# Two-layer hybrid encoder on one core: where the first layer's bias words are requested, how many buffers they have, and when the pads of u are zeroed

## The reference

```python
for layer in range(DEPTH):
    hn = rmsnorm(h, mix_norm_pre[layer])
    proj = jnp.einsum('bsd,de->bse', hn, w_in[layer])
    u, q, k, v = ...                      # 512 columns each
    y_pool = pool_mixer(u, pool_w[layer], pool_scale[layer])
    y_na = neighbourhood_attention(q, k, v, na_rpb[layer])
    mix = jnp.einsum('bse,ed->bsd', jnp.concatenate([y_pool, y_na], axis=-1), w_out[layer])
    h = h + rmsnorm(mix, mix_norm_post[layer])
    hn = rmsnorm(h, ffn_norm_pre[layer])
    f = swiglu(...) if layer % 2 == 0 else moe_swiglu(...)
    h = h + rmsnorm(f, ffn_norm_post[layer])
```

```python
# in neighbourhood_attention, for one row of queries
s = jnp.einsum('bchd,bicjhd->bhcij', q_row, k_nb)
bias = rpb[:, dr[:, None, None], dc[None, :, :]]
p = jax.nn.softmax((s + bias).reshape(...), axis=-1)
```

## Time and profile before

| What | Value |
|---|---|
| Median of 3 runs | 1418.28 us |
| The profiled execution's own time | 1413.12 us |
| Its span on the core | 1411.3 us |
| PE busy | 1309.5 us (93%) |
| DVE, ACT, POOL busy | 417.9, 279.9, 107.0 us |
| DMA, mean over the span | 314 GB/s, 443.40 MB |
| Mean granted PE clock, share of full speed | 0.977 |

### The profile page before, as it was taken

The page is one execution under the profiler, slowest core; times in us unless marked ns, Lnnn a source line. Parts: engine busy times, 40 slices in busy tenths (PEclk is TensorE's granted clock), DMA queues, the critical chain, the costliest instruction groups (busy, mean ns, idle before and its releaser), DMA issues.

```text
span 1411.3 us, 31142 instructions
## 1 busy us (share of the span) xinstructions
PE 1309.5 (93%) x14279; PEld 834.2 (59%) x14279; DVE 417.9 (30%) x567; ACT 279.9 (20%) x413; POOL 107.0 (8%) x239
## 2 busy tenths in 40 slices
PE   5788999999989878999989999997999999999984
PEld 5676999999978865455353354344344355346343
DVE  4587545444565861030020030030020030030022
ACT  4355443343353541000000000000000000000001
POOL 3231500000000215400000000000000000000000
PEclk9899999999989998999999999999999999999997
DMA  9716755555563166999999999998999999999991
GB/s 299 242 61 210 219 194 197 194 182 179 179 216 120 49 239 256 408 403 358 427 426 426 427 426 425 427 425 327 375 426 426 427 426 426 426 426 352 425 426 66
DMA packets 63732, 443.40 MB, mean 314 GB/s; under 512 B 4440, under 2 KB 6496, under 8 KB 39024
## 3 DMA queue, kind: packets, MB, share of 16 engines
q1 hardware_dynamic: 61456, 433.46, 76.6%
q0 software_dynamic: 2144, 7.90, 2.0%
HBM read 440.30 MB, written 1.05 MB: 313 GB/s over the span
## 4 chain that ended last, share of the span: by engine, by line
PE 82%; DMA 8%; DVE 5%; issue 2%; ACT 1%; SPq 1%; POOL 1%; DVEq 0%
PE pd L898 16%; PE pa L889 13%; PE pb L889 13%; PE pc L889 9%; DMA unit<-in_moe_w_down 6%; PE pc L643 3%; PE pc L644 3%; PE pc L645 3%; PE pa L855 3%; PE pd L645 2%; PE pd L644 2%; PE pd L643 2%; DMA rwords_b<-in_na_rpb 2%; PE pa L643 2%; PE pa L644 2%
## 5 line engine op out<-in xcount | busy, mean ns | idle before, releaser
L898 PE MATMUL pd<-unit,hid 128*32 128x256 f32 x4704 | 261.4, 380 | 12.3 <-DMA unit<-in_moe_w_down 11.0
L889 PE MATMUL pa<-unit,xT 128*32 128x448 f32 x2048 | 252.8, 542 | 8.6 <-issue 7.4
L889 PE MATMUL pb<-unit,xT 128*32 128x448 f32 x2048 | 251.9, 541 | 0.0
L898 PEld LDWEIGHTS pd<-unit,hid 128*32 128x32 f32 x4704 | 153.1, 110 | 116.1 <-DMA unit<-in_moe_w_down 17.7
L1187 DVE TENSOR_TENSOR w_lo<-ring,w_hi 128x2048 fp32r<-128x2048 f32 x72 | 169.1, 2350 | 142.3 <-ACT w_hi L991 142.0
L1444 DVE TENSOR_TENSOR hidp<-hid,pa 128x448 f32<-128x448 f32 x16 | 14.9, 933 | 488.1 <-PE pa L889 488.1
L991 ACT ACTIVATE w_hi<-ring 128x2048 fp32r<-128x2048 f32 x72 | 137.3, 1907 | 71.6 <-PE pb L645 54.9
L889 PE MATMUL pc<-unit,xT 128*32 128x448 f32 x1280 | 150.4, 539 | 0.0
L889 PEld LDWEIGHTS pa<-unit,xT 128*32 128x32 f32 x2048 | 71.7, 110 | 129.2 <-issue 125.3
L889 PEld LDWEIGHTS pb<-unit,xT 128*32 128x32 f32 x2048 | 71.9, 110 | 126.4 <-issue 126.4
L643 PE MATMUL pc<-hT_hi,w_hi 128*128 128x256 f32 x448 | 129.4, 289 | 5.1 <-DVE w_lo L1187 4.0
(11 more groups left out here) (254 smaller groups left out, 1364.9 us busy)
## 6 DMA issues: line engine op xcount, KB each, us to landing
unit<-in_moe_w_gate SPq DMA_DIRECT2D x64, 1792.0 KB, 17.6
unit<-in_moe_w_up SPq DMA_DIRECT2D x64, 1792.0 KB, 17.2
unit<-in_moe_w_down SPq DMA_DIRECT2D x64, 1792.0 KB, 23.6
ring<-in_dense_w_gate SPq DMA_DIRECT2D x8, 2048.0 KB, 8.8
ring<-in_dense_w_up SPq DMA_DIRECT2D x8, 2048.0 KB, 8.8
ring<-in_dense_w_down SPq DMA_DIRECT2D x8, 2048.0 KB, 7.7
ring<-in_w_in SPq DMA_DIRECT2D x7, 2048.0 KB, 8.1
ring<-in_w_out SPq DMA_DIRECT2D x4, 2048.0 KB, 13.6
```

The lines of the kernel that those rows point to most:

```text
L889: ins = mm(bank(half, s)[quad(j)], xT[:, dt, Q * s:Q * (s + 1)], w[:, at:at + FJ], start=dt == 0, stop=dt == DT - 1)
L898: ins = mm(down_out[s][quad(j)], e[:, half, s, t, :], w, start=half == t == 0 and s != 2, stop=half == 1 and t == FT - 1, skip_group_check ...
```

## The change

Only the first layer's mixing changes, and lines that both layers share keep their effect in the second layer.

- `rwords` has four buffers: the third, `rwords_c`, lies over `prob` (the probabilities), the fourth, `rwords_d`, over `vv` (v for attention). Each quarter has its own semaphore.
- In the first layer SP asks for all four quarters, sixteen transfers of 192 KB, behind load 1 and ahead of load 2, with no wait for POOL. Load 0 is followed by load 1 at once.
- POOL waits for `hT_ready` ahead of the first quarter.
- The zeroing of `uT` moves from POOL's start to behind the last quarter, with a wait for it, and has a semaphore of its own, `pads_ready`; ACT waits for it ahead of fill 6, DVE ahead of fill 7.

```diff
         rwords = (sb("rwords_a", [P, RW], over="pt23"),
-                  sb("rwords_b", [P, RW], over="ypT_lo"))
+                  sb("rwords_b", [P, RW], over="ypT_lo"),
+                  sb("rwords_c", [P, RW], over="prob"),
+                  sb("rwords_d", [P, RW], over="vv"))
...
+        def word_buffer(layer, quarter):
+            return rwords[quarter % 2 if layer else quarter]
+
         def load_rwords(eng, layer, quarter):
...
-            if n >= 2:
+            if layer:
                 eng.wait_ge(bias_part, 2 * (n - 1))
...
                     load(s0 + j, wi[:, :, c * C4:(c + 1) * C4], DT)
-                    if layer == 0:
-                        load_rwords(sp, 0, j)
+                    if layer == 0 and j == 1:
+                        for quarter in range(4):
+                            load_rwords(sp, 0, quarter)
...
-                    pool.wait_ge(rwords_landed[layer][quarter % 2], 64 * (quarter // 2 + 1))
+                    pool.wait_ge(rwords_landed[layer][quarter], 64)
...
-            link(pool.memset(uT[:, :, :], 0.0))
...
                     pool.wait_ge(cst_landed, 16)
+                    pool.wait_ge(hT_ready, 4)
                     build_bias(0)
+                    pool.wait_ge(bias_part, 8)
+                    pool.memset(uT[:, :, :], 0.0).then_inc(pads_ready, 1)
                     load_gpost(0)
...
                     if g == 5:
+                        act.wait_ge(pads_ready, 1)
                         fill(6, uT[:, 0:2, POOL_PAD:POOL_PAD + S])
...
+                dve.wait_ge(pads_ready, 1)
                 fill(7, uT[:, 2:4, POOL_PAD:POOL_PAD + S])
```

More of the change, by code:

```diff
@@ L260, in hybrid_encoder @@
         router_landed = sem("router_landed")
-        rwords_landed = [[sem(f"rwords_landed{layer}_{i}") for i in range(2)] for layer in range(DEPTH)]
+        rwords_landed = [[sem(f"rwords_landed{layer}_{i}") for i in range(4)] for layer in range(DEPTH)]
         bias_part = sem("bias_part")
+        pads_ready = sem("pads_ready")
         cols_tp = sem("cols_tp")
@@ L338, in load_rwords @@
                 src = bass.AP(rpb.tensor, first - RPB_R * r - (QC - 1), [[1, QC], [1, RW]])
-                eng.dma_start(rwords[n % 2][QC * r:QC * (r + 1), :], src).then_inc(
-                    rwords_landed[layer][quarter % 2], 16)
+                eng.dma_start(word_buffer(layer, quarter)[QC * r:QC * (r + 1), :], src).then_inc(
+                    rwords_landed[layer][quarter], 16)
         def window_delta(eng, link, layer, g, bufs):
@@ L488, in build_bias @@
                 for quarter in range(4):
-                    n = 4 * layer + quarter
-                    pool.wait_ge(rwords_landed[layer][quarter % 2], 64 * (quarter // 2 + 1))
+                    pool.wait_ge(rwords_landed[layer][quarter], 64)
                     for b in range(2):
-                        at = rwords[n % 2][:, 8 - 8 * b:]
+                        at = word_buffer(layer, quarter)[:, 8 - 8 * b:]
                         words = bass.AP(at.tensor, at.offset,
```

## The result

The changed kernel takes 1410.55 us (median of 12 runs, 1407.79 to 1417.77) where the kernel before, beside it, takes 1418.68 (12 runs, 1413.83 to 1423.2): a ratio of 0.995, 95% interval 0.9933 to 0.9966, or 4.8 to 9.5 us less. A second series (e10) gave 1411.95 against 1419.0, a ratio of 0.9964 (0.9946 to 0.9982); one of its 24 runs of the kernel before took 7172.39 us and is not in the ratio. The change makes the kernel faster. The sign was right, but the forecast gain of 1.8 us was about a quarter of the 7 to 8 us between the medians.

The account below looks back on a forecast made before the run. Bias words queued behind weights were taken to bound attention's start. Load 2 at 45.4 plus 1.7 collision gave 47.1; 48.9 - 47.1 = 1.8 us saved, so 1418.28 becomes 1416.5, range 1413.3 to 1420.5.

Parts of the forecast that it names:

- What bounds the kernel: Start of first attention: bias words wait behind weights in SP's queue, so attention starts some 9 us late.
- Step 1: SP's queue, new order: load 1 lands at 23.7, words 27.2 to 37.7, load 2 at 45.4 before any collision.
- The low bound of the step, 44.1: Load 2's earliest landing before any collision: 41.6 plus a quarter of words at the cheap price, 2.5 us.
- The step's upper end, 46.7: Load 2's latest landing before any collision, with the dearest load in place of a middle one.
- Step 2: POOL's bias work ends at 41.3; the zeroing of `uT`, 1.02 us, follows it, hidden behind waits for load 2.
- Step 3: POOL's data for `gpost`, `gpre` and the router meet load 2 and delay it 1.7 us (0 to 3.2), to 47.1.
- L: The landing of load 2, forecast at 47.1, between 44.1 and 49.9; break-even is 48.9.
- Step 4: From load 2's landing through DVE's splits, copy of k and scores: first addition of bias at L + 8.3 = 55.4.
- Step 5: PE works on from fill 4 part 0, regaining full clock: third addition of bias at L + 18.3 = 65.4, before 67.18.
- the sum 48.9 - L: Gain at the third addition of bias, 67.18 - (L + 18.3), forecast as 1.8 us and kept to the end.
- No collision: POOL's data come behind load 2, or words cost 2.5 to 3: L 45.4 to 44.1, 1414.8 to 1413.5 us; chance 0.32.

Follow-up runs that it names:

- e10: The changed kernel unedited, timed again over 12 runs beside the kernel before; 1411.95 us, ratio 0.9964.
- e1: Changed kernel with four buffers but SP's old order, one quarter of bias words behind each of loads 0 to 3; 1418.97 us.
- e2: Changed kernel with all four quarters of bias words behind load 2 instead of behind load 1; 1406.37 us.
- e5: Changed kernel with POOL's requests for `gpost`, `gpre` and the router ahead of the last two quarters; 1416.54 us.
- e7: Changed kernel with the first layer's words fetched from non-overlapping rows of the dense gate weights, same sizes and order; 1411.44 us.
- e9: The kernel of e2 (all words behind load 2), timed over 9 runs beside the kernel before; 1409.48 us, ratio 0.9945.
- e3: Changed kernel with two quarters of words behind load 1 and two behind load 2; 1410.64 us.
- e4: Changed kernel with three quarters of words behind load 1 and one behind load 2; 1414.29 us.
- e6: Changed kernel with two quarters of words behind load 1 and two behind load 3; 1414.2 us.
- e11: The kernel of e3 (two quarters behind load 1, two behind load 2), timed over 10 runs; 1410.09 us, ratio 0.9952.
- e8: The kernel of e2, with DVE splitting the second half of load 2 only behind the first addition of bias; 1415.25 us.

## Why the prediction was wrong, step by step

**What bounds the kernel: right.** The words waited for the weights ahead of them. e1 shows that buffers were not it, and e2 that the landing of load 2 took their place.

**Step 1: the price of load 2; this is the step that failed.** Load 2 was forecast at 45.4 before any collision and landed at 42.5 (42.0 in e10). The term that was mis-sized is load 2's own: 45.4 - 37.7 = 7.7 us behind the last quarter, measured 42.5 - 37.4 = 5.1. The words were forecast from 27.2 to 37.7; the first three landed 1.6 to 1.8 us early, at 25.6, 29.1 and 32.4, because load 1 came at 22.7 (23.7) and the first quarter cost 2.9, and the last one cost 5.0 instead of 3.5. So that its 37.4 met the forecast is luck, and the last quarter and load 2 are better taken together: 10.1 measured, 11.2 forecast. That is 1.1 us of the 2.9; the other 1.8 were earned ahead of the pair.

The rule behind the step was "The total of the queue does not change; its order does", and it is false. Load 5, with the same bytes of SP's queue ahead of it in every kernel, landed at 65.5 before and at 61.2 in the changed kernel. It landed at 60.5 to 61.4 in the other kernels with all words in one row (e2, e5, e7, e9, e10) and at 62.7 to 65.4 where the row is split up (e1, e3, e4, e6, e11). Only e8 does not fit, 63.1 with one row. The prices came from landings, and a landing waits for the latest of sixteen shares: before, load 2 had words ahead of it and behind it, fourteen of its shares had landed by 34.8, and the last came at 38.2. The low bound of the step, 44.1, varied only the price of a quarter; it did not let the load's own price fall when its neighbour changes, though the earlier trace rows had loads at 6.6 and 8.6 side by side. (The step's upper end, 46.7, does not come out of its own terms: 1.0 for the dearest load makes 46.1 or 47.1.)

**Step 2, POOL: right.** The bias was over at 40.3 (41.3 forecast), the zeroing began at 40.32 (41.3), the first quarter was taken up at 25.84 (27.2).

**Step 3, the collision: the mechanism is right, its place was missed.** The 1.7 us were not paid: load 2 landed at 42.5, 1.2 us after POOL's first request at 41.27, ahead of its data. e5, where they do meet, pays 2.9. There turns went by rows, a third of the bytes for the load, so had 1.6 us of load 2 been left, an estimate by that count is 3.2 us and not an even share's 1.7. The error follows from step 1: with load 2 at 42.5 nothing is left to overlap. Of the 47.1 - 42.5 = 4.6 us by which L was missed, 1.8 are the earlier quarter 2, 1.1 the cheaper pair and 1.7 the collision that did not come.

**Step 4: nearly right.** The first addition stands at L + 8.8 (L + 8.3 forecast): the pair of splits took 4.57 (4.5), the scores 1.43 instead of 1.10. Both began beside a fall of the clock: here it was at half from 47.14 on, throughout the scores, before only from 47.07, behind their start at 46.68.

**Step 5: right.** The second addition followed 5.2 us behind, `turn(0)` took 1.09, and the third stood at L + 18.7 (L + 18.3). With the right L the sum 48.9 - L gives 6.4; at the third addition 6.0 were measured. The medians lie 8 and 7 us apart in the two series; the 1 to 2 us beyond the sum are within their intervals and have no cause shown.

**The range.** The rival "No collision" ended at 1413.5 with L = 44.1. Cheaper words and an absent collision were in it, at a chance of 0.32, and that is nearest to what came; its end was set by the same false rule, and so was the low end of the range.

## What to carry to other kernels

A transfer's price in a busy queue is not its own: the same 2 MB cost 5.1 to 8.6 us here by their landings, and what stands behind it counts (2 us or more) as well as what stands ahead. A landing shows when the last share came, so set beside it what the bytes take at the rate of a quiet window (5.5 us here). When transfers of another form are moved together, count the borders between the two forms before and after, and leave the low end of the range open for every border that goes. And when a wait of one thing is moved onto another, place the thing that is now needed first ahead of all: e2 did that with one list, and its attention starts 3 us earlier.

## What the runs showed of the hardware

- A load lands with the last of sixteen completions, and one of them can be late alone: load 2 had fifteen by 34.2 us in e3 and by 34.4 in e6, the last at 37.5 and 36.0. In e3, with words behind it, the last fifteen rows went one after another at 0.14 to 0.29 us each, against 0.09 among loads.
- Words moved at 233 GB/s, a load at 380 (changed kernel, 24 to 33 and 36 to 40 us). In the changed kernel and in e7 quarters landed 3.3 to 3.5 us apart, whether their source rows overlap or not, but for the last one, 5.0 and 3.8 behind the one before.
- Two queues took turns row by row: 208 and 210 packets in 3 us, of 4 KB and 2 KB (e5).
- DVE and POOL hold each other up. A split takes 2.29 us alone and 3.40 beside POOL's additions (in e2, 3.45), a pair of additions of POOL 2.85 alone and 4.90 beside a split; e8, with the split moved away, has 2.85 where e2 has 4.91. The Trainium skill (SBUF — State Buffer, section SBUF: two separate sides) describes a port pair that DVE and POOL hold one at a time; the rows agree: 2.85 and 2.29 make 5.14, and POOL's pair took 4.90.
- The clock granted to PE was at half from 47.14 to 53.97 in the changed kernel, where PE idled from 44.6 to 49.8, and stayed at full in e2, where it idled for 0.91 us at that place.
